# Even mixer: the second and third out piece as three products of split operands, the norm's vector folded into the weights, and all of token tile 0 ahead of tile 1

## The reference, cut to what matters

```
def _even_mixer(x, w_in, conv_w, conv_b, dt_bias, a_log, d_skip, norm_g, w_out):
    h = x @ w_in
    z, xbc, dt_raw, q, k, v = _split(h, [...])
    ...
    y = _ssd_scan(xs, dt, a, bs, cs)                      # state-space part, 1024 wide
    y = (y + d_skip[:, None] * xs).reshape(bsz, s, SSD_INNER)
    y = _rms_norm(y * jax.nn.silu(z), norm_g)             # norm over 1024, vector norm_g
    sb = _stick_breaking_attention(q, k, v)               # attention part, 512 wide
    return jnp.concatenate([y, sb], axis=-1) @ w_out      # w_out is 1536 x 1024
```

## Time and profile before

| | |
|---|---|
| Median of three runs | 2087.65 us (2086.98 to 2088.06) |
| The profiled execution | 2087.62 us, its span 2085.9 us |
| Mean granted TensorE clock | 0.998 of full speed |
| Busy: TensorE, VectorE, ScalarE | 2063.1 us (99%), 1686.7 us (81%), 1411.0 us (68%) |
| Plain float32 out products of the even mixer (L1129) | 96 records, from 136.2 to 182.8 us |
| ScalarE between 149.24 and 162.94 us | idle 13.70 us |

### The profile page before, as it was taken

The page is one execution under the profiler, slowest core; times in us unless marked ns, Lnnn a source line. Parts: engine busy times, 40 slices in busy tenths (PEclk is TensorE's granted clock), DMA queues, the critical chain, the costliest instruction groups (busy, mean ns, idle before and its releaser), DMA issues.

```text
span 2085.9 us, 30649 instructions
## 1 busy us (share of the span) xinstructions
PE 2063.1 (99%) x9954; PEld 1683.6 (81%) x9954; DVE 1686.7 (81%) x2270; ACT 1411.0 (68%) x1891; POOL 140.2 (7%) x132
## 2 busy tenths in 40 slices
PE   9999999999999999999999999999999999999999
PEld 8976888868887887888867888888888888888887
DVE  5766998749987656446768999999999999999997
ACT  5754785437885544444535888888888888888886
POOL 1001101002100001111111000000000000000000
PEclk9999999999999999999999999999999999999999
DMA  8417995627984555451434999999999999999995
GB/s 295 153 66 284 402 411 171 240 103 276 403 316 152 201 230 225 185 198 41 162 142 184 402 377 382 375 387 377 381 384 370 386 375 389 376 386 378 365 402 210
DMA packets 88550, 601.59 MB, mean 288 GB/s; under 512 B 10545, under 2 KB 10609, under 8 KB 19985
## 3 DMA queue, kind: packets, MB, share of 16 engines
q1 hardware_dynamic: 79616, 569.88, 69.5%
q0 software_dynamic: 8704, 30.08, 4.8%
q10 hardware_dynamic: 144, 0.52, 0.1%
HBM read 585.12 MB, written 15.32 MB: 288 GB/s over the span
## 4 chain that ended last, share of the span: by engine, by line
PE 92%; DVE 5%; ACT 1%; issue 1%; POOL 0%; DMA 0%; DVEq 0%; ACTq 0%; POOLq 0%
PE bank L532 22%; PE bank L528 22%; PE bank L529 21%; PE bank L519 4%; PE bank L521 4%; PE bank L520 4%; PE bank L1129 2%; PE bank L1605 2%; PE bank L2723 1%; PE bank L3265 1%; PE bank L457 1%; PE bank L1681 1%; DVE pj_lo L565 1%; PE bank L463 1%; PE bank L1724 0%
## 5 line engine op out<-in xcount | busy, mean ns | idle before, releaser
L2037 DVE TENSOR_TENSOR gu_lo<-ffw_gu,gu_hi 128x1024 fp32r<-128x1024 f32 x620 | 754.4, 1236 | 91.0 <-ACT gu_hi L1827 77.2
L1827 ACT CAST gu_hi<-ffw_gu 128x1024 fp32r<-128x1024 f32 x620 | 647.8, 1052 | 88.0 <-PE bank L532 38.9
L528 PE MATMUL bank<-gu_lo,xg_hi 128*128 128x512 f32 x1152 | 462.6, 402 | 0.0
L529 PE MATMUL bank<-gu_hi,xg_hi 128*128 128x512 f32 x1152 | 449.1, 390 | 0.0
L2037 DVE TENSOR_TENSOR dn_lo<-ffw_d,dn_hi 128x1024 fp32r<-128x1024 f32 x293 | 357.2, 1230 | 22.3 <-ACT dn_hi L1835 14.5
L1835 ACT CAST dn_hi<-ffw_d 128x1024 fp32r<-128x1024 f32 x304 | 319.3, 1056 | 57.3 <-PE bank L532 50.1
L532 PE MATMUL bank<-gu_hi,xg_lo 128*128 128x512 f32 x1152 | 356.8, 391 | 0.0
L528 PE MATMUL bank<-dn_lo,hidt_hi 128*128 128x512 f32 x652 | 254.5, 390 | 0.7 <-ACT hidt_hi L1864 0.5
L529 PE MATMUL bank<-dn_hi,hidt_hi 128*128 128x512 f32 x652 | 253.9, 389 | 0.0
L532 PEld LDWEIGHTS bank<-gu_hi,xg_lo 128*128 128x128 f32 x1152 | 216.3, 188 | 46.4
L529 PEld LDWEIGHTS bank<-gu_hi,xg_hi 128*128 128x128 f32 x1152 | 217.1, 188 | 40.3
(11 more groups left out here) (476 smaller groups left out, 2728.7 us busy)
## 6 DMA issues: line engine op xcount, KB each, us to landing
ffw_gu<-in_gate_up_m SPq DMA_DIRECT2D x288, 1024.0 KB, 7.1
ffw_d<-in_down_m SPq DMA_DIRECT2D x144, 1024.0 KB, 8.8
pieces<-in_pieces SPq DMA_DIRECT2D x70, 1024.0 KB, 7.0
ffw_gu<-in_gate_up_ff SPq DMA_DIRECT2D x22, 1024.0 KB, 6.8
ffw_d<-in_down_ff SPq DMA_DIRECT2D x11, 1024.0 KB, 8.8
h<-token_sums POOLq DMA_DIRECT2D x3, 1024.0 KB, 7.2
norm_vec<-in_ln_g POOLq DMA_DIRECT2D x4, 512.0 KB, 4.6
norm_vec<-in_ln_b POOLq DMA_DIRECT2D x4, 512.0 KB, 6.3
```

The source lines that it names most:

```text
L528: nc.tensor.matmul(bank, a_hi, b_lo, start=start, stop=False)
L529: nc.tensor.matmul(bank, a_hi, b_hi, start=False, stop=False)
L1827: nc.scalar.copy(gu_hi[:, 2 * k:2 * k + 2, :], ffw_gu[:, blk["slot"], 2 * k:2 * k + 2, :])\
L2037: return V.tensor_tensor(out, x, hi.bitcast(F32), ALU.subtract)
```

## The change

The second and third out piece are multiplied as three products of split operands. Each of their eight 128x1024 blocks of weights is multiplied by the norm's vector and rounded on ScalarE (`even_out_hi_scalar`), and VectorE makes the rest, in place in the piece's slot (`even_out_lo_vector`); the high parts lie in free places of the arena. The transposed features are rounded on ScalarE (`even_features_scalar`) and their rest made on VectorE (`even_features_vector`), without the norm's vector. The two transposed pieces use banks 4, 5 and 6, 7, so that all 16 transposes can go in a row. TensorE takes tile 0 for both pieces, then tile 1. A semaphore of a later stage is renamed (`sg_turned_hi` to `features_hi`) and its counts are moved on; that is left out here.

```diff
@@ -960,6 +961,12 @@
     sb_take, sb_pass, sb_w, sb_wT = (sb_flat[:, i * 6 * P:(i + 1) * 6 * P].rearrange("p (b i t) -> p b i t", b=2, i=3)
                                      for i in range(4))
     decay = sb_flat[:, 0:16 * P].rearrange("p (s i l) -> p s i l", s=4, i=4)
+    late_at, token_at, decay_at, conv_at, mix_at = ARENA - 2 * D, 15384, 17432, 8192, 13312
+    OUT_HI_AT = ((late_at, late_at + D, token_at, token_at + D), (conv_at, decay_at, decay_at + D, mix_at))
+    ev_out_hi = [[parts_at(f"ev_out{k}_hi{c}", arena_at + 4 * at, D) for c, at in enumerate(ats)] for k, ats in enumerate(OUT_HI_AT)]
+    ev_out_lo = [parts_at(f"ev_out{k}_lo", pieces_at + 4 * PW * (even_out[k + 1] % PSLOTS), 4, D) for k in range(2)]
+    ev_feat_hi, ev_feat_lo = ([parts_at(f"ev_feat{k}_{part}", at + 4 * i * 4 * S, 4, S) for k, at in enumerate((xt_at, arena_at + 4 * 10240))]
+                              for i, part in enumerate(("hi", "lo")))
...
@@ -1111,10 +1118,7 @@
     def even_turn_tensor(pe, k):
 
         for c0 in (0, 2):
-            g = 2 * k + c0 // 2
-            bank = psum[(6 if k == 0 else 4) + c0 // 2]
-            if k == 2:
-                pe.wait_ge(sem("mixt_read"), g - 1)
+            bank = psum[(4 if k == 1 else 6) + c0 // 2]
             for c in (c0, c0 + 1):
                 for j in range(T):
                     at = (2 * (c - c0) + j) * P
@@ -1123,12 +1127,26 @@
                                                ident)
             last.then_inc(sem("mixt_turned"), 1)
 
-    def even_out_tensor(pe, k, j, half):
+    def even_out_tensor(pe, j, half):
 
         for c in range(4):
-            last = nc.tensor.matmul(psum[2 * j + half], ev_mixT[:, k, c, TILES[j]],
-                                    piece_ap(even_out[k])[:, c, half * 512:(half + 1) * 512],
-                                    start=(k == 0 and c == 0), stop=(k == 2 and c == 3))
+            last = nc.tensor.matmul(psum[2 * j + half], ev_mixT[:, 0, c, TILES[j]],
+                                    piece_ap(even_out[0])[:, c, half * 512:(half + 1) * 512], start=(c == 0), stop=False)
+        return last
+
+    def even_out_split_tensor(pe, k, j, half):
+
+        bank, cols, first = psum[2 * j + half], slice(half * 512, (half + 1) * 512), j == 0 and half == 0
+        for c in range(4):
+            if first and c % 2 == 0:
+                pe.wait_ge(sem("features_hi"), FEATURES_HI["ev"] + 2 * k + c // 2 + 1)
+            if first:
+                pe.wait_ge(sem("so_split"), OUT_SPLIT["ev"] + 4 * k + c + 1)
+            high_products(bank, ev_feat_hi[k][:, c, TILES[j]], (ev_out_hi[k][c][:, cols], ev_out_lo[k][:, c, cols]), False)
+        if first:
+            pe.wait_ge(sem("mixt_read"), 2 * (k + 1) + 2)
+        for c in range(4):
+            last = low_product(bank, ev_feat_lo[k][:, c, TILES[j]], ev_out_hi[k][c][:, cols], k == 1 and c == 3)
         return last
 
     def even_tensor(pe):
@@ -1172,23 +1190,21 @@
         piece_wait(pe, even_out[0])
         for i, (j, half) in enumerate(((1, 0), (1, 1), (0, 0), (0, 1))):
             read_wait(pe, "ev", half, EV_N - j)
-            last = even_out_tensor(pe, 0, j, half)
+            last = even_out_tensor(pe, j, half)
             for g, r in ssd_step(4 * EV_N + i):
                 ssd_tensor(pe, g, r)
         last.then_inc(sem("out_piece"), 1)
         pe.wait_ge(sem("mix_ready"), 1)
         for k in (1, 2):
             even_turn_tensor(pe, k)
-        for k in (1, 2):
-            piece_wait(pe, even_out[k])
-            pe.wait_ge(sem("mixt_read"), 2 * k + 2)
-            for j in range(T):
+        for j in range(T):
+            for k in range(2):
                 for half in range(2):
-                    last = even_out_tensor(pe, k, j, half)
-                    if k == 2:
+                    last = even_out_split_tensor(pe, k, j, half)
+                    if k == 1:
                         last.then_inc(sem("out_half"), 1)
-            if k == 1:
-                last.then_inc(sem("out_piece"), 1)
+                if j == 1 and k == 0:
+                    last.then_inc(sem("out_piece"), 1)
...
@@ -1263,6 +1279,20 @@
             fade(2, 7)
         if r == 2:
             fade(3, 6)
+
+    def even_out_hi_scalar(act, k, cs):
+
+        piece_wait(act, even_out[k + 1])
+        for c in cs:
+            nc.scalar.mul(ev_out_hi[k][c], piece_ap(even_out[k + 1])[:, c, :], par["ssd_norm"][:, k, c:c + 1])\
+                .then_inc(sem("so_hi_ready"), 1)
+
+    def even_features_scalar(act, k):
+
+        for b in range(2):
+            act.wait_ge(sem("mixt_turned"), 2 * (k + 1) + b + 1)
+            nc.scalar.copy(ev_feat_hi[k][:, 2 * b:2 * b + 2, :], psum[4 + 2 * k + b].rearrange("p (c t) -> p c t", c=2))\
+                .then_inc(sem("features_hi"), 1)
 
     def even_scalar(act):
         A = nc.scalar
@@ -1309,6 +1339,8 @@
                             .then_inc(sem("mixt_read"), 1)
                 for g, r in ssd_step(at):
                     ssd_scalar(act, g, r)
+                    if (g, r) == (1, 1):
+                        even_out_hi_scalar(act, 0, (0, 1))
                 if k == 3:
                     even_evacuate_scalar(act, n)
                 if at + 1 in SSD_AT:
@@ -1323,6 +1355,17 @@
             act.wait_ge(sem("gated"), j + 1)
             A.activation(zs[:, j, :], ev_mix[:, j, SB_W:], ACT.Square, scale=SSD_INNER ** -0.5,
                          accum_out=sq[:, j:j + 1]).then_inc(sem("squared"), 1)
+            if j == 0:
+                act.wait_ge(sem("ev_weights"), 4 * SSD_G)
+                even_out_hi_scalar(act, 0, (2, 3))
+                even_out_hi_scalar(act, 1, (0,))
+                act.wait_ge(sem("ev_diag"), 4 * SSD_G)
+                even_out_hi_scalar(act, 1, (1,))
+            else:
+                even_out_hi_scalar(act, 1, (2,))
+        for k in range(2):
+            even_features_scalar(act, k)
+        even_out_hi_scalar(act, 1, (3,))
         act.wait_ge(sem("mix_ready"), 1)
         first_weights_scalar(act, "m0")
...
@@ -1386,6 +1429,21 @@
         dve.wait_ge(sem("ev_z_ready"), j + 1)
         y = ev_mix[:, j, SB_W:]
         vlink(V.tensor_tensor(y, y, zs[:, j, :], ALU.mult), sem("gated"))
+
+    def even_out_lo_vector(dve, k, cs):
+
+        for c in cs:
+            dve.wait_ge(sem("so_hi_ready"), OUT_SPLIT["ev"] + 4 * k + c + 1)
+            V.scalar_tensor_tensor(out=ev_out_lo[k][:, c, :], in0=piece_ap(even_out[k + 1])[:, c, :],
+                                   scalar=par["ssd_norm"][:, k, c:c + 1], in1=ev_out_hi[k][c].bitcast(F32),
+                                   op0=ALU.mult, op1=ALU.subtract).then_inc(sem("so_split"), 1)
+
+    def even_features_vector(dve, k):
+
+        for b in range(2):
+            dve.wait_ge(sem("features_hi"), FEATURES_HI["ev"] + 2 * k + b + 1)
+            V.tensor_tensor(ev_feat_lo[k][:, 2 * b:2 * b + 2, :], psum[4 + 2 * k + b].rearrange("p (c t) -> p c t", c=2),
+                            ev_feat_hi[k][:, 2 * b:2 * b + 2, :].bitcast(F32), ALU.subtract).then_inc(sem("mixt_read"), 1)
 
     def even_vector(dve):
         vlink(V.memset(xp[:, :, :, 0:CONV_K - 1], 0.0))
@@ -1427,9 +1485,10 @@
                 for g, r in ssd_step(at):
                     if r == 0 and g:
                         ssd_vector(dve, g, r)
-        for at in (4 * EV_N, 4 * EV_N + 1):
-            for g, r in ssd_step(at):
-                ssd_vector(dve, g, r)
+        even_out_lo_vector(dve, 0, (0, 1))
+        ssd_vector(dve, 1, 3)
+        even_out_lo_vector(dve, 0, (2,))
+        ssd_vector(dve, 1, 4)
         for j in range(T):
             dve.wait_ge(sem("squared"), j + 1)
             vlink(V.tensor_scalar(sq[:, j:j + 1], sq[:, j:j + 1], RMS_EPS, None, ALU.add))
@@ -1441,11 +1500,11 @@
                 root_wait_vector()
             vlink(V.tensor_scalar(ev_mix[:, j, SB_W:], ev_mix[:, j, SB_W:], rstd[:, j:j + 1], None, ALU.mult),
                   *([sem("mix_ready")] if j else []))
-        for k in (1, 2):
-            for b in range(2):
-                V.wait_ge(sem("mixt_turned"), 2 * k + b + 1)
-                V.tensor_tensor(ev_mixT[:, k, 2 * b:2 * b + 2, :], psum[4 + b].rearrange("p (c t) -> p c t", c=2),
-                                over(par["ssd_norm"][:, k - 1, 2 * b:2 * b + 2], 2, S), ALU.mult).then_inc(sem("mixt_read"), 1)
+        even_out_lo_vector(dve, 0, (3,))
+        even_out_lo_vector(dve, 1, (0,))
+        for k in range(2):
+            even_features_vector(dve, k)
+        even_out_lo_vector(dve, 1, (1, 2, 3))
         first_weights_vector(dve, "m0")
```

More of the change, by code:

```diff
@@ L274, in build @@
     ROUTER = {"m0": 0, "m1": 1, "m2": 2}
+    OUT_SPLIT, FEATURES_HI = {"ev": 0, "sg": 8}, {"ev": 0, "sg": 4}
     NEXT = {"m0": "od", "m1": "sg", "ff": "da"}
@@ L302, in build @@
     for k in range(3):
-        released[sg_out[k]] = ("so_split", 4 * (k + 1))
+        released[sg_out[k]] = ("so_split", OUT_SPLIT["sg"] + 4 * (k + 1))
     def piece_wait(eng, n):
@@ L2968, in sg_tensor @@
```

(8 more changed lines are left out.)

## The result

| | |
|---|---|
| Changed kernel, median of five runs | 2098.52 us (2097.09 to 2099.50) |
| Kernel before, beside it, median of five | 2087.09 us (2086.90 to 2088.06) |
| Ratio, 95% interval | 1.0055 (1.0044 to 1.0066), 11.4 us slower |
| Forecast | 2097.0 us (2094.5 to 2099.5), slower |
| Its profiled execution | 2098.7 us, span 2097.0 (before 2085.9), clock 0.995 |

What follows compares the result with a forecast made beforehand. TensorE, busy 99% of the span, was taken as the bound. Transposes 13.1 us later, 0.8 more for transposes, 5.4 less and 0.9 more for products: +9.4 on 2087.6 gives 2097.0 us (2094.5 to 2099.5).

Steps and rivals of the forecast that it cites:

- The wait: ScalarE's third-piece multiplies hold the square of tile 1, so TensorE starts the transposes 13.1 us after ending at 152.74.
- The clock: TensorE resumes at half clock after the stand: 16 transposes take 3.4 us, products lose 0.9 us.
- The products: Second and third out piece on TensorE: 96 products at 0.23 us, 22.1 against 27.47, 5.4 us less.
- Carried unchanged to the end: The stage's +9.4 us, products ending at 192.2 against 182.8, reaches the program's end unchanged: 2097.0 us.
- a shift at the end that differs from the one at 192: Sign that the prediction is wrong; every later stage was to shift by the same amount as the stage's end.
- The third: Rival: third out piece lands before about 147, products end at 176.6; -6.2 us, 2081.4; chance 0.05.
- The fourth: Rival: third block's loads late, or token-row transfers meet later weight loads; 2.5 us more, 2099.5; chance 0.08.
- 20 us of cover: Third block's weights: issued at 186.7, some 10 us to land, used at 217.7; costs nothing.

Runs made afterwards that it cites:

- third_own_place: Changed kernel with the third out piece in one slot of the experts' gate-up weights, issued behind the last projection piece: 2092.6 us, ratio 1.0029.

## Why the prediction was right, and where its sizes were off

*The wait.* Right. Forecast: third piece whole at 160.4, square at 162.6, mix_ready at 165.7, TensorE at 165.8. Traced: 160.6, 162.73, 165.9, 165.97. The two multiplies took 1.10 each where I had 1.05. Moving the multiplies behind the square took 9.4 us away, and an early piece moved the end of the stage by 16 us, with the orders of ScalarE, VectorE and TensorE as they were: it is the wait for the piece, in that place of ScalarE's order, and neither the extra work nor the order of the tiles. One row bore less than I read from it: ScalarE's idle time before 162.94 is put down to "issue", so the row alone does not show when the next transfer landed.

*The clock.* Right, and shown by a run that only fills the stand: half clock behind it, forecast at 1.65 us for the transposes and 0.9 for the products, in the trace 1.49 (3.69 against 2.20 behind the filled stand) and 0.83 for four products at 0.43 and one at 0.27, together 2.3 where the forecast has 2.2 to 2.6.

*The products.* Mis-sized by 0.2: 0.232 each, 22.3 us where I had 22.1. The stage came to +9.94 instead of +9.4; the rest of the half microsecond is the start of the transposes (0.17 later) and their 3.69 for 3.4, less 0.1 on the products at half clock.

*Carried unchanged to the end.* Wrong by 1.2 us, and most of what the forecast missed in the trace. The forecast named a shift at the end that differs from the one at 192 as a sign of being wrong, and the sign is there. The shift is +9.94 behind the stage, +11.13 behind the first expert stage, +9.54 at 464.9, +11.1 from 1129 on. The last two steps are low-clock stretches elsewhere. In the kernel before, one follows the 1.74 us stand ahead of 435.00; the changed kernel stands there just as long, ahead of 446.19, and its clock stays at 1.00. At 1124 to 1130 it has a longer one than the kernel before:

```profile
1124.00:1127.00 3.00, 3.00 (x16) 3.00 (x16) 2.60 (x9) 1.04 (x1) 0.89 (x2) 0.50 0.00 0
1127.00:1130.00 3.00, 3.00 (x16) 3.00 (x16) 1.57 (x9) 0.22 (x1) 0.63 (x1) 0.50 0.85 326
```

The kernel before, in the same work:

```profile
1114.00:1118.00 4.00, 4.00 (x23) 4.00 (x23) 3.51 (x12) 1.04 (x1) 1.47 (x3) 0.60 0.00 0
1118.00:1121.00 3.00, 3.00 (x29) 3.00 (x27) 1.95 (x10) 0.22 (x1) 0.16 (x1) 0.97 1.01 393
```

These steps of 1.6 us, one each way, cancel here by luck. They come and go in the experiments in no relation to what was edited: the kernel before with nothing but the tile order has both, the changed kernel with 57 matmuls neither. The times of one and the same kernel do it too: of the 60 executions of the kernel before beside the experiments, 23 took 2085.3 to 2086.1 us and 37 took 2086.8 or more, and none lies between. That this is the same thing as the steps is not shown, but it makes differences between medians of under some 1.6 us hard to put down to an edit. The first step, in the first expert stage, is on ScalarE, which waits longer for a gate-up load:

```profile
235.65 1.05 ACT L1886 CAST gu_hi<-ffw_gu 128x1024 fp32r<-128x1024 f32 x1 [1.97 <-DMA ffw_gu<-in_gate_up_m]
...
246.85 1.05 ACT L1886 CAST gu_hi<-ffw_gu 128x1024 fp32r<-128x1024 f32 x1 [3.87 <-DMA ffw_gu<-in_gate_up_m]
```

Before, its longest such wait was 2.76 us. From 230 to 260 the transfers of that stage run near 420 GB/s without a gap, as they do in the kernel before from 220 to 250. The stage lost between 1.1 and 2.5 us in each of the split kernels whose loads did not meet the table's writes, against 0.2 gained with the tile order alone. What in the split kernels sets that amount stays open; the late release of the second piece was tried and is not it.

*Rivals.* The third (the piece in time) was priced at -6.2 us. As a stage that is what happens when one makes it true (-6.0), but as a time it is not: 2092.6 and 2086.8 first, and 2082.8 only once SP's order fits. I had priced a stage and carried it, the same step that failed above. The fourth (late loads, or transfers of the token rows meeting weight loads) was dismissed by 20 us of cover for the *third block's* weights. Those came in time in the changed kernel, but ScalarE waited longer for a load behind them, and the 1.2 us are lost in that stretch; in the experiments the meeting decided, and the transfers that had no cover were the small ones.

## What to carry to other kernels

When an instruction that waits for a transfer is put into an in-order engine, look at what stands behind it, not at what it feeds: here a 1 us square, which reads nothing of the late piece, waited 14.6 us, and TensorE behind it 13.2. Let the late operand be consumed last on every engine, or load it earlier; and if it is loaded earlier, move the whole queue with it, since a transfer that now waits holds back all loads behind it and can bunch them onto small dependent transfers. Here the gain of one stage became a gain of the program only when the loads of the next stage were ordered for it.

## What the runs showed of the hardware that was not expected

The wait behind a small indirect write to memory was 1.4 to 2.3 us where the DMA engines were otherwise quiet (share 0.02 to 0.06), 8.0 us with 5.7 MB of weights issued 15 us ahead of it and 3 MB more behind them (share 1.0), and 14.6 in the run third_own_place. A chain of such steps is therefore as sensitive to the load order as any weight tile. And TensorE's clock stayed at 1.00 through a 13 us wait that was filled with matmuls whose results nobody reads; mix_ready came 0.3 us later in that trace, from what isn't shown. A stand of 1.74 us in the same place was followed by the half clock in one kernel and not in the other.
